# Gate tiles 10 and 11 of a two-block transformer kernel, moved from behind the attention into the early chunks by seven products

## What is computed

```python
proj = h @ w_in                       # 1024 x (8*512 + 8 + 2048)
(q_a, k_a, v_a, z_a, q_b, k_b, v_b, z_b, f_logit, g_logit) = split(proj)
y_a = (stick_breaking(q_a, k_a, v_a) * silu(z_a)) @ w_o_sb
cum = cumsum(log_sigmoid(f_logit + b_forget))
y_b = (forgetting_attention(q_b, k_b, v_b, cum) * silu(z_b)) @ w_o_fox
gates = sigmoid(g_logit + b_gate)     # two halves of 1024
merged = gates[0] * y_a + gates[1] * y_b
x = x + gate * (merged @ w_out)       # then the norm and the second block
```

## Time and profile before

| | |
|---|---|
| median of three runs | 1243.8 us |
| the profiled execution | 1243.3 us, span 1241.5 us |
| TensorE busy | 1213.8 us (98%) |
| TensorE weight loads | 1040.3 us (84%) |
| VectorE busy | 857.2 us (69%) |
| ScalarE busy | 653.9 us (53%) |
| GpSimd busy | 428.9 us (35%) |
| TensorE clock granted | 1.00 throughout |
| DMA, mean over the span | 174 GB/s |

### The profile page before, as it was taken

One profiled execution on the slowest core, in us unless ns is written; L12 is line 12 of the kernel. 1 busy time (PEld: TensorE's weight loads), 2 busy tenths in 40 slices (PEclk: granted clock), 3 DMA queues, 4 the chain that ended last, 5 costly groups with the idle time before them and its releaser, 6 DMA issues.

```text
span 1241.5 us, 22880 instructions
## 1 busy us (share of the span) xinstructions
PE 1213.8 (98%) x9270; PEld 1040.3 (84%) x9270; DVE 857.2 (69%) x1342; ACT 653.9 (53%) x1027; POOL 428.9 (35%) x330
## 2 busy tenths in 40 slices
PE   6999999999999999999998989999999999999999
PEld 6798999876767777777787768788878999999999
DVE  4288887789653166697638766456668888878974
ACT  6555463677765524463455554454435555556452
POOL 5552000422333636456333034540555223333000
DMA  9853332666986993667321018851542556656554
GB/s 389 356 200 127 116 103 102 222 238 206 268 205 162 245 318 131 210 165 168 91 103 37 4 69 307 259 137 24 149 125 92 164 187 187 187 170 210 184 185 144
DMA packets 42182, 215.53 MB, mean 174 GB/s; under 512 B 5080, under 2 KB 5208, under 8 KB 28128
## 3 DMA queue, kind: packets, MB, share of 16 engines
q1 hardware_dynamic: 34272, 140.74, 32.2%
q0 software_dynamic: 4608, 28.31, 12.1%
q10 hardware_dynamic: 3200, 45.04, 9.9%
HBM read 206.72 MB, written 63.98 MB: 218 GB/s over the span
## 4 chain that ended last, share of the span: by engine, by line
PE 81%; DVE 9%; ACT 4%; DMA 2%; issue 2%; POOL 1%; SPq 0%; DVEq 0%; ACTq 0%; POOLq 0%
PE banks L664 79%; PE banks L671 2%; DMA weights<-in_stream 2%; DVE arena L2598 1%; POOL weights_low L3283 1%; ACT weights_high L1488 1%; DVE arena L2595 1%; DVE arena L2600 1%; DMA h<-in_stream 1%; DVE h_low L2340 1%; POOL arena L3342 0%; ACT arena L1637 0%; ACT arena L1542 0%; DVE arena L2430 0%; DVE weights_low L2340 0%
## 5 line engine op out<-in xcount | busy, mean ns | idle before, releaser
L3283 POOL TENSOR_TENSOR weights_low<-weights,weights_high 128x512 fp32r<-128x512 f32 (+1 forms) x216 | 308.5, 1459 | 500.0 <-ACT weights_high L1488 500.0
L664 PE MATMUL banks<-h_high_low,weights_high 128*128 128x512 f32 (+1 forms) x696 | 243.3, 350 | 0.7 <-DVE weights_low L2470 0.5
L664 PE MATMUL banks<-h_high_low,weights_low 128*128 128x512 f32 (+1 forms) x696 | 235.8, 339 | 0.0
L664 PE MATMUL banks<-h_low,weights_high 128*128 128x512 f32 (+1 forms) x696 | 235.7, 339 | 0.0
L1488 ACT ACTIVATE weights_high<-weights 128x2048 fp32r<-128x2048 f32 (+1 forms) x85 | 126.8, 1504 | 73.6 <-PE banks L664 59.1
L664 PEld LDWEIGHTS banks<-h_high_low,weights_high 128*128 128x128 f32 x696 | 131.1, 188 | 19.8 <-issue 3.7
L664 PEld LDWEIGHTS banks<-h_low,weights_high 128*128 128x128 f32 x696 | 131.1, 188 | 16.6 <-issue 2.4
L664 PEld LDWEIGHTS banks<-h_high_low,weights_low 128*128 128x128 f32 x696 | 131.1, 188 | 16.1
L664 PE MATMUL banks<-arena 64*64 64x64 f32 (+6 forms) x1800 | 116.4, 263 | 1.3 <-POOL arena L3342 0.7
L664 PEld LDWEIGHTS banks<-arena 64*64 64x64 f32 (+3 forms) x1800 | 84.6, 147 | 23.6 <-issue 16.5
L3361 POOL TENSOR_TENSOR weights_low<-weights,weights_high 128x512 fp32r<-128x512 f32 x32 | 48.4, 1534 | 112.8 <-ACT weights_high L1500 112.8
(11 more groups left out here) (463 smaller groups left out, 3292.9 us busy)
## 6 DMA issues: line engine op xcount, KB each, us to landing
weights<-in_stream SPq DMA_DIRECT2D x66, 1024.0 KB, 6.0
up_sums<-in_up POOLq DMA_DIRECT2D x16, 1024.0 KB, 9.6
weights<-up_sums SPq DMA_DIRECT2D x64, 256.0 KB, 3.0
weights<-in_up SPq DMA_DIRECT2D x48, 256.0 KB, 2.9
sums_kept<-in_down POOLq DMA_DIRECT2D x16, 704.0 KB, 7.6
arena<-in_ada SPq DMA_DIRECT2D x8, 1024.0 KB, 11.8
weights<-sums_kept SPq DMA_DIRECT2D x9, 704.0 KB, 4.2
sums_kept<-in_down ACTq DMA_DIRECT2D x8, 704.0 KB, 6.2
```

Source lines behind the costliest of these rows:

```text
L664: ins = nc.tensor.matmul(o, lhsT, rhs, start=start, stop=stop, skip_group_check=skip)
L3283: nc.gpsimd.tensor_tensor(lo_of(c)[:, cols], raw_of(c)[:, cols], hi_of(c)[:, cols].bitcast(F32), ALU.subtract).then_inc(sem("weights_split ...
```

## The change

- `EARLY_TILES` gets ("g", 5) between `za` 1 and `qb` 0, so there are twelve early chunks. Gate tiles 10 and 11 are written over the place of `kb` and stored to HBM by ScalarE (512 KB); VectorE waits for that store before it writes `kb` 0. The stream of chunks in HBM is ordered to match, and `EARLY_G` is 10, so `project` behind the attention has no tile left.
- Behind the attention ScalarE loads 512 KB and 1024 KB of gates, waits for both, and has six gates (10 to 15) to make from loaded tiles.
- `forget_gates` and `forget_sums` run earlier, with a work place of their own, and the store of `nF` too.
- TensorE waits for all early moves at step 2 (LAG) of the attention and not at step 1; `g` 8 and 9 go to banks 2 and 3.
- VectorE waits for gate m before the product with tile m, not for all 16 ahead of the first.
- ScalarE splits one chunk of the first stage in two halves with a move between them, and in `between_blocks` the split goes ahead of the high part.

```diff
-EARLY_TILES = (("qa", 1), ("ka", 0), ("ka", 1), ("za", 0), ("za", 1), ("qb", 0), ("qb", 1), ("kb", 0), ("kb", 1), ("g", 6), ("g", 7))
+EARLY_TILES = (("qa", 1), ("ka", 0), ("ka", 1), ("za", 0), ("za", 1), ("g", 5), ("qb", 0), ("qb", 1),
+               ("kb", 0), ("kb", 1), ("g", 6), ("g", 7))
 EARLY = len(EARLY_TILES)
-Z_FIRST, EARLY_G = EARLY_TILES.index(("za", 0)), 12
+Z_FIRST, EARLY_G = EARLY_TILES.index(("za", 0)), 10
...
-        gates = [at(512 * m if m < EARLY_G else GATES_AT + 512 * (m - EARLY_G), T) for m in range(16)]
+        gates = [at(512 * m if m < 12 else GATES_AT + 512 * (m - 12), T) for m in range(16)]
+        early_gates = {5: at(8192, 2, T), 6: at(GATES_AT, 2, T), 7: at(GATES_AT + 2 * T, 2, T)}
...
-        z_gate = at(16896, 2, T)
+        z_gate, f_work = at(16896, 2, T), at(22528, 2, T)
...
@@ TensorE
-                if i == 1:
+                if i == LAG:
                     pe.wait_ge(sem("product_moved"), MOVED0)
...
                     if i == 2 * N:
-                        M.use([0, 1, 2, 3])
+                        M.use([2, 3, 0, 1])
                     project("g", 1, KD, h, T, first=SIDE_G + i - 2 * N)
...
@@ ScalarE
             first_high(5, KD)
+            split_weights(0, 2)
             values_out(3, 1)
-            split_weights()
+            split_weights(1, 2)
...
+            forget_gates()
             move(("qa", 1), qa[:, 1, :], scale=HEAD ** -0.5)
             for n, (e, f) in enumerate(EARLY_SEQ):
...
                 if f == R7:
                     early_sum_high(e + 1, R5)
                     early_split(e + 1)
+                    if e >= 2 and EARLY_TILES[e - 2] == ("g", 5):
+                        act.wait_ge(sem("product_moved"), early_moved(e - 2, C12))
+                        act.dma_start(gates_kept[:, 0:2 * T], at(8192, 2 * T)).then_inc(sem("keys_kept"), 16)
+                    if e == 1:
+                        act.wait_ge(sem("nF_ready"), 1)
+                        act.dma_start(nF_kept, f_work[0:HEADS, 1, :]).then_inc(sem("nF_stored"), 16)
...
-                    if e == 0:
-                        forget_gates()
             split_weights()
...
-            act.dma_start(at(GATES_AT, 4 * T), gates_kept).then_inc(sem("keys_kept"), 16)
+            act.dma_start(at(512 * EARLY_G, 2 * T), gates_kept[:, 0:2 * T]).then_inc(sem("keys_kept"), 16)
+            act.dma_start(at(GATES_AT, 4 * T), gates_kept[:, 2 * T:]).then_inc(sem("keys_kept"), 16)
             for m in range(SIDE_G, EARLY_G):
                 gate_out(m)
                 gate_inverse(m)
-            act.wait_ge(sem("keys_kept"), 64)
+            act.wait_ge(sem("keys_kept"), 96)
             for m in range(EARLY_G, 16):
                 link(nc.scalar.activation(gates[m], gates[m], ACT.Exp, scale=-1.0, bias=npar("b_gate", m)))
                 inverse(gates[m]).then_inc(sem("gates"), 1)
...
             def between_blocks(k):
+                split_after(k)
                 act.wait_ge(sem("h_raw"), KD + k + 1)
                 high(h_hi[:, k, :], h_raw[:, k, :], sem("h_hi"))
-                split_after(k)
...
@@ VectorE
                 if f == P2:
+                    if EARLY_TILES[e] == ("kb", 0):
+                        dve.wait_ge(sem("keys_kept"), 48)
                     early_moves(stt(early_tile(e, 0, 0), o, by, k1, ALU.mult, ALU.add))
...
                     if e == 0:
                         gate_columns()
-                    elif e == 1:
                         forget_sums()
...
-            dve.wait_ge(sem("gates"), 16)
             for m in range(KD):
                 o = M.full(dve, ("oa", m))
+                dve.wait_ge(sem("gates"), m + 1)
                 tt(gates[m], o, gates[m], ALU.mult).then_inc(M.out(("oa", m)), 1)
...
                     o = M.full(dve, ("ob", m))
+                    dve.wait_ge(sem("gates"), KD + m + 1)
                     tt(gates[KD + m], o, gates[KD + m], ALU.mult).then_inc(M.out(("ob", m)), 1)
```

More of the change, by code:

```diff
@@ L557, in early_tile @@
             if key == "g":
-                return gates[2 * c + half][:, TH * side:TH * (side + 1)]
+                return early_gates[c][:, half, TH * side:TH * (side + 1)]
             to = {"qa": qa, "ka": ka, "za": gated["a"], "qb": qb, "kb": kb}[key]
@@ L1645, in silu @@
                 if tag == "a":
-                    if m < 2:
-                        act.wait_ge(sem("nF_ready"), 1)
                     act.wait_ge(sem("product_moved"), early_moved(Z_FIRST + m // 2, C12))
@@ L1695, in forget_gates @@
             def forget_gates():
-                act.wait_ge(sem("keys_kept"), 32)
                 o = F.full(act, "f")
-                fx, fa = z_gate[0:HEADS, 0, :], z_gate[0:HEADS, 1, :]
+                fx, fa = f_work[0:HEADS, 0, :], f_work[0:HEADS, 1, :]
                 nc.scalar.activation(fx, o[0:HEADS, :], ACT.Identity, scale=-1.0, bias=npar("b_forget")[0:HEADS, :])\
@@ L1790, in stick_step @@
                     act.wait_ge(sem("product_moved"), MOVED0)
-                    act.dma_start(gates_kept, at(GATES_AT, 4 * T)).then_inc(sem("keys_kept"), 16)
+                    act.dma_start(gates_kept[:, 2 * T:], at(GATES_AT, 4 * T)).then_inc(sem("keys_kept"), 16)
                 if i == 2:
-                    act.wait_ge(sem("keys_kept"), 48)
+                    act.wait_ge(sem("nF_stored"), 16)
+                    act.wait_ge(sem("keys_kept"), 64)
                 if i % 2 == 0 and 2 <= i <= N:
@@ L1810, in stick_step @@
                     nc.scalar.activation(w, w, ACT.Exp).then_inc(sem("stick_w"), 1)
-                if i == 1:
-                    act.wait_ge(sem("nF_ready"), 1)
-                    act.dma_start(nF_kept, nF[0:HEADS, :]).then_inc(sem("nF_stored"), 16)
                 if i == 2:
@@ L1816, in stick_step @@
                 if i == 4:
-                    act.wait_ge(sem("nF_stored"), 16)
                     act.dma_start(nF_bc[0], nF_kept[0:2, :].partition_broadcast(P)).then_inc(sem("nF0_loaded"), 16)
@@ L2539, in forget_sums @@
             def forget_sums():
-                fx, fa = z_gate[0:HEADS, 0, :], z_gate[0:HEADS, 1, :]
+                fx, fa = f_work[0:HEADS, 0, :], f_work[0:HEADS, 1, :]
                 dve.wait_ge(sem("f_ln"), 1)
                 link(stt(fx, fx, 0.0, fa, ALU.max, ALU.add))
-                nc.vector.tensor_tensor_scan(nF[0:HEADS, :], ones(T, HEADS), fx, 0.0, ALU.mult, ALU.add)\
+                nc.vector.tensor_tensor_scan(fa, ones(T, HEADS), fx, 0.0, ALU.mult, ALU.add)\
                     .then_inc(sem("nF_ready"), 1)
@@ L2585, in stick_step @@
                 n = i - LAG
+                if n == 0:
+                    dve.wait_ge(sem("nF_stored"), 16)
                 if 0 <= n < N:
@@ L3507, in lay_stream @@
         if i == 5:
-            parts.append(by_gates[EARLY_G // 2:])
-    parts.append(by_gates[:EARLY_G // 2])
+            parts.append(by_gates[6:])
+        if i == 3:
+            parts.append(by_gates[5:6])
+    parts.append(by_gates[:5])
     parts.append(lay_chunks(np.asarray(a["w_o_sb"])[0], 512))
@@ L3564 @@
     nF_kept = nc.dram_tensor("nF_kept", [HEADS, T], F32, kind="Internal").ap()
-    gates_kept = nc.dram_tensor("gates_kept", [P, 4 * T], F32, kind="Internal").ap()
+    gates_kept = nc.dram_tensor("gates_kept", [P, 6 * T], F32, kind="Internal").ap()
     sums_kept = nc.dram_tensor("sums_kept", [4, DOWN_PAIRS, P, DOWN_W], F32, kind="Internal").ap()
```

1 line of the change is left out of this document (removed).

## The result

The changed kernel took **1261.9 us** (median; 1260.9 to 1265.7) against 1244.0 for the kernel before: ratio 1.0140, 95% interval 1.0120 to 1.0161. It is slower, as forecast, but by 17.9 us where 9.8 were forecast, and outside the range, which ended at 1258.0.

The account below looks back on a forecast made before the run. TensorE's queue of matmuls was taken as the bound (81% of the chain). Early stage +9.1 us plus +0.7 behind the attention gave +9.8 on 1243.3, so 1253.1 us; range 1245.5 to 1258.0.

Parts of the forecast that it names:

- Added chunk: Early stage: a twelfth chunk of 84 matmuls of 256 columns adds 10.0 us, all on TensorE's path.
- The hole at 130.65: Early chunks: TensorE's 0.49 us wait for a low part goes as `forget_sums` moves a chunk earlier, -0.5 us.
- The hole at 89.33: Before the early chunks: TensorE's 0.42 us hole goes as the half split starts GpSimd about 1.2 us earlier, -0.4 us.
- Removed tiles: Between last values and `oa`: `g` 10 and 11 gone, -11.35 us, but `oa` starts after 1.4 us idle; L2672's 1.2 us wait goes.
- First wait: Before `ob`'s first chunk: late gates load and six gates delay its split; TensorE idles 5.1 us, then loses 1.7 us more.
- Second wait: ScalarE's wait inside the `merged_hi` loop: last accumulations, issued after the second `ob` chunk, land at 448 us, bounds 446 and 451.
- From the landing to the end of the first `wo` tile: After the last accumulations land: VectorE steps, split, GpSimd's low part and two k of TensorE take 13.8 us, ending at 461.8.
- the seam: From VectorE's last product with `gated` to the start of the third `wo` tile: 70.0 us before, +0.7 forecast.
- rival C: Behind the attention: gates load takes 17.7 us, everything behind it 4.6 us later, 1257.7 us; chance 0.10.
- A: Rival: neither new wait behind the attention decides, -3.1 us in all, 1240.2 us, faster; chance 0.08.
- B: Rival: `ob` starts late but the accumulations are in by 441 as before, +3.5 us, 1246.8 us; chance 0.14.
- The rule about 512 columns: TensorE's removed tiles: at the skill's 131 ns per matmul they are 6.3 us, a loss from the start; trace says 234 ns.

Follow-up runs that it names:

- the run with additional matmuls: Changed kernel with 22 additional matmuls of 512 columns before `ob` and 22 before its last tile, results unused: 1261.9 us, ratio 1.0136.
- the first two experiments: Each on the changed kernel: accumulations issued one chunk earlier, 1253.3 us; split of the first `ob` chunk ahead of ScalarE's wait for the gates load, 1255.1 us.
- all cures and early low parts: Changed kernel with accumulations a chunk earlier, first `ob` split ahead of gates, copies behind `merged_hi`, low parts of `gated` 0 to 3 before VectorE's last product: 1240.7 us.
- both waits cured and the copies behind: Changed kernel with accumulations a chunk earlier, first `ob` split ahead of the gates, and copies behind the eight `merged_hi`: 1242.4 us, ratio 0.9976.
- the first experiment: Changed kernel with each pair of GpSimd's accumulations issued one chunk earlier: 1253.3 us, ratio 1.0066 to the kernel before.
- with eleven and with twelve chunks, cured alike: Eleven: kernel before plus small moves, copies behind `merged_hi`, early low parts, 1241.9 us. Twelve: changed kernel, these plus earlier accumulations and first `ob` split, 1240.7 us.
- both edits: Changed kernel with accumulations one chunk earlier and the split of the first `ob` chunk ahead of the gates: 1245.0 us, ratio 1.0003.

## Why the prediction was right and where it fell short

The way, the two waits and the engines behind them were right. The step that failed is the second wait and what follows from it: the last accumulations were priced to land at 448 and came 3.0 us later, the chain of steps from there to the end of the first `wo` tile was priced at 13.8 us and took 17.4, and the stages behind were priced at nothing.

**Added chunk.** Forecast 10.03 us, or 9.5 with the hole that goes: measured 9.2. The hole at 130.65 is gone. The hole at 89.33 is not: 0.44 us at 89.95. The half split came earlier and the low parts with it, but TensorE still waits. That step was wrong by its 0.4 us.

**Removed tiles.** `oa` was to start 1.4 us after the last values: 1.48. No wait for L2672, and none in front of the third `wo` tile: right.

**First wait.** Gates landed, counted from VectorE's last product as zero: 14.3 us after it; I had 13.8 (410.5 - 396.69). First `ob` matmul: 29.3 after, forecast 28.9 (425.6); idle time 5.27, forecast 5.1. The load of 1 MB took 13.2 us, beside the 512 KB and GpSimd's accumulations. The Trainium skill, "DMA: Bandwidth & Descriptors", section "Bandwidth", gives 6.15 us for 1 MB on its own, as the busy time of a transfer that GpSimd issued; by that the prediction would have had 1.2 us for this hole. No run here has this load on its own, so none contradicts the page; the figure doesn't fit a load beside others.

**Second wait.** Last pair issued 39.0 after, forecast 39.4. Landed 54.3 after, forecast 51.3 (448), upper bound 54.3 (451): **3.0 us** short, at the very bound. I counted 11.7 us, the median of the pair's two DMAs, from the first issue. But ScalarE is let go by the later of the two, which the second wait in the earlier trace rows had shown: 14.9 us from the first issue, the figure of the upper bound. Here it is 15.4.

**From the landing to the end of the first `wo` tile.** Forecast 13.8 us, measured 478.29 - 460.85 = 17.4: **3.6 us** short, the largest miss. I had followed ScalarE's split and GpSimd's low part, and priced VectorE's steps at 0.6 to 0.7 us. But those steps, 17 of them from 462.06 to 476.34, run in part beside GpSimd's low part of the first `wo` chunk (466.70 to 473.07), and four of them are then longer, by 3.1 us in all: two sums take 1.29 and 1.07 us, two low parts 1.77, in place of 0.69:

```profile
466.52 0.69 DVE L2682 TENSOR_TENSOR arena<-banks,arena 128x512 f32<-128x512 f32 x1
467.24 1.29 DVE L2685 TENSOR_TENSOR arena<-arena 128x512 f32<-128x512 f32 x1
468.46 1.77 DVE L2342 TENSOR_TENSOR merged_low<-arena,merged_high_b 128x512 fp32r<-128x512 f32 x1
470.15 0.68 DVE L2682 TENSOR_TENSOR arena<-banks,arena 128x512 f32<-128x512 f32 x1
470.87 1.07 DVE L2685 TENSOR_TENSOR arena<-arena 128x512 f32<-128x512 f32 x1
471.86 1.77 DVE L2342 TENSOR_TENSOR merged_low<-arena,merged_high_b 128x512 fp32r<-128x512 f32 x1
```

The trace of the kernel before has the same beside the same low part of GpSimd:

```profile
450.89 1.79 DVE L2340 TENSOR_TENSOR merged_low<-arena,merged_high_b 128x512 fp32r<-128x512 f32 x1
```

So VectorE and not GpSimd ended this chain (TensorE's two waits at 473.68 and 475.70 name its low parts). The half clock of `ob`'s last tile isn't the cause: with that tile at full clock, in the run with additional matmuls, the way from the landing (459.58) to the end of the first `wo` tile (476.96) is 17.4 us too. The matmuls behind the two waits ran at half the clock: the second tile took 6.0 us in place of 5.6. That is the remaining 0.4.

3.0 + 3.6 + 0.4 = 7.0 us, and the seam is 77.8 where 70.7 was forecast. The rest of the way from 9.8 to 17.65 is 0.6 us at the start of the trace and 0.1 in the early chunks.

**Behind the seam.** The forecast had no term here ("the shift stays"). The profiles have one in nearly every kernel, the tail against the 774.9 us before: +3.2 changed, +6.7 and +6.2 in the first two experiments, +3.4 in the kernel before with late accumulations alone, +0.9 with all cures and early low parts. The second block's wait for `h_low` goes from 0 to 2.9 us; it is 1.2 us or more where ScalarE, 10 to 12 us ahead of it, waits 3.4 to 5.0 us for a weight chunk, and under 0.2 where that wait is 2.7 to 3.4. With one profile for each kernel, what makes that chunk late stays open.

**The range** was too narrow, because its upper end had the slow load (rival C) and the late landing one at a time, and the chain of steps behind it and the tail without any bound at all.

**Rivals.** A didn't happen. Its sum holds where its condition was made by other code: with both waits cured and the copies behind, the seam is 57.5 where A's terms give 57.7 (70.0 - 11.35 + 1.4 - 1.2 - 1.1). B needed the last pair to land as before; the first experiment made that so, and its seam (65.9) is that of B (70.0 - 5.6 = 64.4) within 1.5. C did not happen: 13.2 us for the load, not 17.7, and ScalarE's wait for it 6.87 us, not over 10.

**The rule about 512 columns** (Trainium skill, "TensorE: Matmul & The Clock Gate", section "Back-to-back issue gap", about 131 ns in a stream) has no support in any run here: with eleven and with twelve chunks, cured alike, the seams differ by 11.2 us for 48 matmuls, 233 ns each.

## What to carry to other kernels

Work that is taken out from between two stages was also a cover: list for each engine what it does under it, in its own order, and ask when the next stage's first operand is ready if the work is gone. Steps that are tied to a count of chunks, as the accumulations were here, move when a chunk is taken out, though no line of them is in the diff; and a wait in the middle of a loop should stand behind everything in its queue that someone else is waiting for. Whatever the seven products for eight gain here (1 to 2 us by the profiles, not shown by the times) could be there only after the order behind it had been made anew.

## What the runs showed of the hardware

In this stretch VectorE's sum or low part of two operands in SBUF (128x512) takes 0.69 us alone, 1.07 to 1.77 beside GpSimd's low parts, and once 4.56 us: it began beside four of them back to back (440.50 to 446.07) and ended 0.6 us after the last:

```profile
442.07 4.56 DVE L2685 TENSOR_TENSOR arena<-arena 128x512 f32<-128x512 f32 x1
446.55 0.68 DVE L2682 TENSOR_TENSOR arena<-banks,arena 128x512 f32<-128x512 f32 x1
```

L2682 beside it, with one operand in PSUM, stays at 0.68 to 0.69 us throughout. The Trainium skill, "SBUF — State Buffer", section "Who interferes with whom", says that an operation of VectorE with two SBUF inputs contends with one of GpSimd that reads SBUF, and one with at most one SBUF input, outside the modes that use both port pairs, doesn't: the trace agrees with both halves. I hadn't used it in the forecast, and it would have raised the term that missed most.

Behind a hole of about 5 us TensorE was granted the lower of its two clock levels (1.2 in place of 2.4 GHz): behind the first, twelve starts of 512 columns in a row came 0.427 us apart (436.41 to 441.53) in place of 0.234 before it rose. Shorter holes show both: those of 1.88 us in `wo` (both edits) and of 2.94 us in the second block (first experiment) had the lower clock behind them, those of 1.48 us in front of `oa` and of 1.88 us in the second block of the changed kernel did not. Keeping TensorE busy in the two holes of 5 us kept the clock up there and the time where it was, since the next waits, for the accumulations and for VectorE, took up what the slower matmuls lost.

A load of 1 MB of weights took 4.7 us from issue to landing when it was asked for ahead of the eight copies between sums, and 19.6 to 20.4 us beside them.
